# Memory's norm moved behind its transposes, its gain loaded as 8 rows and turned by TensorE, the rotary angles computed on POOL

## The reference

```python
def rms_norm(x, g):
    y = x * lax.rsqrt(jnp.mean(x * x, axis=-1, keepdims=True) + EPS)
    return y * g

def memory_attention(q_flat, mem_n, w_kv):
    kv = (mem_n @ w_kv).reshape(b, n_mem, 2, M_HEADS, M_HEAD_DIM)
    k, v = kv[:, :, 0], kv[:, :, 1]
    ...

mem_n = rms_norm(mem, g_mem)          # once
for l in range(DEPTH):
    h = rms_norm(x, g_mix[l])
    # h @ w_in[l], rotary(q, positions), rotary(k, positions), memory_attention(qm, mem_n, w_mem_kv[l]) ...
```

## Time and profile before

| what | value |
|---|---|
| median of 3 runs | 1711.03 us (1710.94 to 1711.79) |
| the profiled execution's own time | 1710.64 us |
| its span (first to last instruction) | 1708.9 us |
| TensorE busy | 1690.4 us |
| VectorE busy | 1338.8 us |
| ScalarE busy | 1167.7 us |
| POOL busy | 69.8 us |

### The profile page before, as it was taken

How to read it: one execution, slowest core, us unless ns; L and a number is a source line. 1 busy time by engine, 2 the same in 40 slices (tenths; PEclk the granted TensorE clock), 3 DMA queues, 4 the chain that set the end, 5 groups by cost and what they waited for, 6 DMA issues and landing times.

```text
span 1708.9 us, 26645 instructions
## 1 busy us (share of the span) xinstructions
PE 1690.4 (99%) x8790; PEld 1430.2 (84%) x8790; DVE 1338.8 (78%) x1390; ACT 1167.7 (68%) x1362; POOL 69.8 (4%) x91
## 2 busy tenths in 40 slices
PE   9999999999999999999999999999999999999997
PEld 8977889999988877888888888888888888888886
DVE  7675575455457664879998989999899999899998
ACT  6565644444444655578888787787878888887876
POOL 3000000000000000020000000000000000000020
PEclk9999999999999999999999999999999999999999
DMA  9533468666556433699999999999999999999994
GB/s 348 177 112 113 152 228 302 182 193 184 184 160 197 134 113 113 234 360 395 372 376 392 377 376 395 367 385 392 370 385 381 358 403 373 375 396 367 382 354 163
DMA packets 169910, 496.46 MB, mean 291 GB/s; under 512 B 15584, under 2 KB 17680, under 8 KB 169344
## 3 DMA queue, kind: packets, MB, share of 16 engines
q1 hardware_dynamic: 165168, 480.57, 77.6%
q0 software_dynamic: 4688, 15.18, 2.8%
HBM read 482.56 MB, written 13.13 MB: 290 GB/s over the span
## 4 chain that ended last, share of the span: by engine, by line
PE 91%; ACT 3%; DVE 3%; issue 1%; DMA 1%; SPq 0%; DVEq 0%; POOL 0%; ACTq 0%
PE ps L1879 85%; PE ps L2360 1%; ACT probs L1137 1%; PE ps L2161 1%; PE ps L2144 1%; ACT probs L1129 1%; PE ps L2131 1%; DVE wlo L1340 1%; DVE row_max L1555 1%; ACT whi L997 1%; DVE probs L1550 1%; DMA raw<-in_w_mem_kv 1%; PE ps L2133 0%; PE ps L2367 0%; ACT gates L1007 0%
## 5 line engine op out<-in xcount | busy, mean ns | idle before, releaser
L1340 DVE TENSOR_TENSOR wlo<-raw,whi 128x1024 fp32r<-128x1024 f32 (+1 forms) x768 | 910.7, 1218 | 273.0 <-ACT whi L997 252.0
L997 ACT ACTIVATE whi<-raw 128x1024 fp32r<-128x1024 f32 (+1 forms) x768 | 801.1, 1058 | 324.4 <-PE ps L1879 310.0
L1879 PE MATMUL ps<-whi,xg_hi 128*128 128x512 f32 x896 | 351.9, 393 | 0.5 <-DVE xg_lo L1769 0.5
L1879 PE MATMUL ps<-wlo,xg_hi 128*128 128x512 f32 x896 | 348.9, 389 | 0.0
L1879 PE MATMUL ps<-whi,xg_lo 128*128 128x512 f32 x896 | 348.7, 389 | 0.0
L1879 PEld LDWEIGHTS ps<-whi,xg_hi 128*128 128x128 f32 x896 | 168.2, 188 | 36.7 <-DVE wlo L1340 3.0
L1879 PEld LDWEIGHTS ps<-wlo,xg_hi 128*128 128x128 f32 x896 | 168.2, 188 | 35.3
L1879 PEld LDWEIGHTS ps<-whi,xg_lo 128*128 128x128 f32 x896 | 168.3, 188 | 33.9
L1879 PE MATMUL ps<-whi,actm_hi 128*128 128x512 f32 x448 | 175.8, 392 | 0.0
L1879 PE MATMUL ps<-wlo,actm_hi 128*128 128x512 f32 x448 | 174.6, 390 | 0.0
L1879 PE MATMUL ps<-whi,actm_lo 128*128 128x512 f32 x448 | 174.4, 389 | 0.0
(11 more groups left out here) (342 smaller groups left out, 2189.8 us busy)
## 6 DMA issues: line engine op xcount, KB each, us to landing
raw<-in_w_down_exp SPq DMA_DIRECT2D x216, 512.0 KB, 6.3
raw<-in_w_gate_exp SPq DMA_DIRECT2D x210, 512.0 KB, 5.6
raw<-in_w_up_exp SPq DMA_DIRECT2D x120, 512.0 KB, 5.7
raw<-in_w_in SPq DMA_DIRECT2D x72, 512.0 KB, 3.6
vM<-in_w_up_exp SPq DMA_DIRECT2D x56, 512.0 KB, 5.6
kM<-in_w_up_exp SPq DMA_DIRECT2D x48, 512.0 KB, 5.7
raw<-in_w_gate_dense SPq DMA_DIRECT2D x28, 512.0 KB, 3.7
raw<-in_w_up_dense SPq DMA_DIRECT2D x28, 512.0 KB, 3.9
```

What stands on the lines that cost most here:

```text
L997: s.activation(whi[n % SPLIT][:, 0:w], raw[tile(key)][:, 0:w], ACT.Copy).then_inc(chunk_hi, 1)
L1340: v.tensor_tensor(wlo[n % SPLIT][:, 0:w], raw[tile(key)][:, 0:w], whi[n % SPLIT][:, 0:w].bitcast(F32), ALU.subtract).then_inc(chunk_split, 1)
L1879: ins = mm(o, lhsT, rhs, start=start and i == 0, stop=stop and i == 2, skip_group_check=True)
```

## The change

- Memory is transposed as it is loaded, without its norm. The gain is put on as the transposed memory is copied out of PSUM, where a column of `g_mem` is one number per partition. For this `g_mem` is loaded as 8 rows of 128 (4 KB, issued by ACT), transposed by TensorE and copied by DVE to `mem_gain`.
- The rstd of a memory token is put on later: on the values as one number per partition (`values_out`), on the keys as a row `mem_rows`, the same in every partition, which TensorE makes from two diagonal matrices (`mem_diag`, made by DVE from the rstd) and a matrix of ones (`rstd_rows`). `keys_out` moves from ACT to DVE and multiplies by that row. The row is spilled and brought back as the transposed memory is.
- The first chunk's products go in another order: all high x high first, which wait only for the high part, then high x low, then low x high (`first_keys`).
- ACT and DVE take memory's piece ahead of the chunk's high and low part. ACT squares memory's second half and all of `x` after four chunks and ahead of the other four; DVE makes memory's means and the two diagonals after the fourth low part and ahead of the fifth.
- `reduced_angles` moves to POOL, with three of its steps cut in two (19 instructions). POOL's order becomes: identity, positions and frequencies, mask, angles, memory's two powers, x's gain, the small loads, x's powers. x's gain now waits for the two diagonals.
- `idle_products` and the two clearings go; 13 + 7 warming products become 5 + 2 + 2 + 5.

```diff
@@ build_tally
     transposed(("memT",))
+    psum(("mem_rows",), 0)
@@ SP
             for t in range(NT):
                 sp.dma_start(normed[:, t, :], A["mem"][0, P * t:P * (t + 1)]).then_inc(mem_loaded[t], 16)
-            sp.dma_start(gain[:, :], A["g_mem"].partition_broadcast(P)).then_inc(mem_gain_loaded, 16)
...
+                if key == ("qa", 0, 3):
+                    wait_read(sp, ("mem_rows",))
+                    sp.dma_start(rows_spill, mem_rows[:, :]).then_inc(mem_saved, 16)
@@ POOL
-            rstd_of(0)
             (loads of positions and frequencies)
+            (mask: one memset, two affine_selects)
+            reduced_angles()
+            rstd_of(0, mem_rstd)
+            load_gain(1, A["g_mix"][0])
             (small loads, router's weights)
-            (mask: one memset, two affine_selects)
-            load_gain(1, A["g_mix"][0])
@@ POOL, reduced_angles: pool_done adds a wait for the instruction just issued
+                pool_done(nc.gpsimd.tensor_copy(pos_f[:, :], pos_i[:, :]))
+                for t in range(NT):
+                    pool_done(nc.gpsimd.tensor_scalar(ang[:, 2, t, :], freqs[:, :], pos_f[:, t:t + 1], None, ALU.mult))
+                for i, quarter in enumerate((0.0, 0.25)):
+                    pool_done(nc.gpsimd.tensor_scalar(ang[:, 3 + i, :, :], ang[:, 2, :, :], 0.15915494309189535, quarter, ALU.mult, ALU.add))
...
+                pool_done(nc.gpsimd.tensor_scalar(k, k, ROUND, None, ALU.add))
+                pool_done(nc.gpsimd.tensor_scalar(k, k, ROUND, None, ALU.subtract))
+                pool_done(nc.gpsimd.tensor_scalar(ang_part[:, :, :], k, -TWO_PI_HI, None, ALU.mult))
+                pool_done(nc.gpsimd.tensor_tensor(r, ang_part[:, :, :], angle, ALU.add))
...
@@ ACT
+            eng.dma_start(mem_gain_rows[:, :], A["g_mem"].rearrange("(k p) -> k p", p=P)).then_inc(mem_gain_loaded, 16)
+            def mem_hi(i):
+                wait_full(eng, ("memT", i // 2, "area"))
+                for k in range(2 * i, 2 * (i + 1)):
+                    c = TOK * (k % 4)
+                    ins = s.activation(memT_hi[:, k, :], ps[i // 2][:, c:c + TOK], ACT.Copy, scale=mem_gain[:, k:k + 1])
+                ins.then_inc(hi_copied, 1)
...
+            mem_square(0)
+            eng.wait_ge(mem_gain_ready, 1)
+            for i, key in enumerate(opening[0:4]):
+                mem_hi(i)
                 hi_of(key)
+            mem_square(1)
             eng.wait_ge(x_loaded, 16)
+            eng.wait_ge(meansq_ready, NT)
             for t in range(NT):
                 for half in range(2):
                     square(x, half, t)
-            hi_of(opening[6])
-            keys_out(0)
-            hi_of(opening[7])
+            for key in opening[4:]:
+                hi_of(key)
@@ DVE
-            norm(0, normed, normed)
+            v.memset(mem_ones[:, :], 1.0).then_inc(mem_ones_ready, 1)
+            eng.wait_ge(mem_gain_turned, 1)
+            v.tensor_copy(mem_gain[:, :], ps[2][:, 0:KD]).then_inc(mem_gain_ready, 1)
+            eng.wait_ge(mem_gain_ready, 1)
             for i, key in enumerate(opening[0:4]):
+                (two scalar_tensor_tensor: memT_lo = ps * mem_gain - memT_hi)
                 lo_of(key)
-                transposed_piece(("memT",), i, memT_hi, memT_lo)
-            reduced_angles()
+            for t in range(NT):
+                norm_mean(0, t)
+            eng.wait_ge(constants, 3)
+            for t in range(NT):
+                eng.wait_ge(rstd_ready, t + 1)
+                v.tensor_scalar(mem_diag[:, t, :], ident[:, :], mem_rstd[:, t:t + 1], None, ALU.mult).then_inc(norm_done, 1)
             for key in opening[4:6]:
                 lo_of(key)
             wait_full(eng, ("memT", 1, "area"))
             norm(1, x, normed)
+            wait_full(eng, ("mem_rows",))
+            v.tensor_copy(mem_rows[:, :], area(("mem_rows",))[:, 0:TOK]).then_inc(psum_free[0], 1)
+            wait_read(eng, ("mem_rows",))
+            keys_out(0)
             for key in opening[6:] + mixer_chunks(0)[0:2]:
                 lo_of(key)
@@ DVE, layer 0, ahead of the dense block (keys_out(1) was on ACT between two high parts)
+                    lo_of(dense_first[2])
+                    eng.wait_ge(mem_back, 48)
+                    keys_out(1)
+                    lo_of(dense_first[3])
@@ TensorE
             pe.wait_ge(constants, 3)
-            keep_busy(13, ps[3][:, 0:P])
-            pe.wait_ge(tiles_cleared, 2)
-            idle_products()
-            transposes(("memT",), 0)
-            keep_busy(7, ps[3][:, 0:P])
-            for c in range(4):
+            keep_busy(5, ps[3][:, 0:P])
+            pe.wait_ge(mem_gain_loaded, 16)
+            nc.tensor.transpose(ps[2][:, 0:KD], mem_gain_rows[:, :], ident[0:KD, 0:KD]).then_inc(mem_gain_turned, 1)
+            keep_busy(2, ps[3][:, 0:P])
+            transposes(("memT",), 0, [0])
+            keep_busy(2, ps[3][:, 0:P])
+            transposes(("memT",), 0, [1])
+            keep_busy(5, ps[3][:, 0:P])
+            first_keys()
+            for c in range(1, 4):
                 wait_piece(("memT",), c)
                 mem_keys(0, c)
...
                     mem_values(l, c)
+                    if l == 0 and c == 0:
+                        rstd_rows()
```

More of the change, by code:

```diff
@@ new lines, in _ @@
+            reduced_angles()
+            rstd_of(0, mem_rstd)
+            load_gain(1, A["g_mix"][0])
+            for l in range(DEPTH):
+                pool.dma_start(g_lat[:, l, 0:Q_RANK], A["g_q_lat"][l].partition_broadcast(P)).then_inc(small_loaded, 16)
+                pool.dma_start(g_lat[:, l, Q_RANK:], A["g_kv_lat"][l].partition_broadcast(P)).then_inc(small_loaded, 16)
+                pool.dma_start(sink[:, l, :], A["sink"][l].partition_broadcast(P)).then_inc(small_loaded, 16)
+            pool.dma_start(wr[:, :, :], A["w_router"][0].rearrange("(k p) e -> p k e", p=P)).then_inc(router_loaded, 16)
@@ L1024, in transposed, with mem_square @@
                     transposed_part(name, a, dst)
-            for t in range(NT):
+            eng.dma_start(mem_gain_rows[:, :], A["g_mem"].rearrange("(k p) -> k p", p=P)).then_inc(mem_gain_loaded, 16)
[5 more added lines that the diff above has]
+                ins.then_inc(hi_copied, 1)
+            def mem_square(t):
                 eng.wait_ge(mem_loaded[t], 16)
@@ new lines, in _ @@
+            eng.wait_ge(mem_gain_ready, 1)
+            for i, key in enumerate(opening[0:4]):
+                eng.wait_ge(hi_copied, tl.after("hi_copied", ("memT", i)))
+                for k in range(2 * i, 2 * (i + 1)):
+                    c = TOK * (k % 4)
+                    ins = v.scalar_tensor_tensor(memT_lo[:, k, :], ps[i // 2][:, c:c + TOK], mem_gain[:, k:k + 1],
+                                                 memT_hi[:, k, :].bitcast(F32), ALU.mult, ALU.subtract)
+                ins.then_inc(hT_split, 1)
+                lo_of(key)
@@ L1989, in mem_values, with first_keys, rstd_rows @@
                                   banks(("memv", l), 512), 2, 512, c == 0, c == 3))
+            def first_keys():
+                key = ("memk", 0, 0)
+                n = slot(key) % SPLIT
+                o = area(("memk", 0))
+                for i, (w, rows) in enumerate(((whi, memT_hi), (whi, memT_lo), (wlo, memT_hi))):
+                    if i == 0:
+                        pe.wait_ge(chunk_hi, chunk_no(key, 0) + 1)
+                        pe.wait_ge(hi_copied, tl.after("hi_copied", ("memT", 0)))
+                    elif i == 1:
+                        wait_piece(("memT",), 0)
+                    else:
+                        wait_chunk(key)
+                    for kk in range(2):
+                        for j in range(4):
+                            ins = mm(o[:, TOK * j:TOK * (j + 1)], w[n][:, 512 * kk + P * j:512 * kk + P * (j + 1)],
+                                     rows[:, kk, :], start=i == 0 and kk == 0 and j % 2 == 0, stop=False,
+                                     skip_group_check=True)
+                used(ins)
+            def rstd_rows():
+                key = ("mem_rows",)
+                wait_free(pe, key)
+                pe.wait_ge(mem_ones_ready, 1)
+                pe.wait_ge(norm_done, NT)
+                for t in range(NT):
+                    ins = mm(area(key)[:, P * t:P * (t + 1)], mem_ones[:, :], mem_diag[:, t, :], start=True, stop=True)
+                ins.then_inc(psum_full[0], 1)
             def wait_piece(name, i):
```

120 lines of the change are left out of this document (53 added, 67 removed).

## The result

The changed kernel takes 1716.18 us (median of 9 runs, 1715.42 to 1716.91), the kernel before 1711.74 (9 runs, 1710.63 to 1712.12): ratio 1.0028, 95% interval [1.0020, 1.0037], slower by 4.4 us. The profiled execution took 1716.25 us, its span is 1714.5, against 1710.64 and 1708.9. The forecast was 1714.3, with slower a little less likely than no change: the time came out 1.9 above it, inside the range.

The account below looks back on a forecast made before the run. TensorE, busy 99% of the span, was taken as the bound, so c6's start decides: T 23.8 plus 12.2 gives 36.0 against 32.70, 3.3 late. 1710.64 becomes 1713.9, plus 0.39 is 1714.3 us; 8-in-10 range 1708.5 to 1720.

Parts of the forecast that it names:

- first product: TensorE's first real product in the opening, claimed at 8.4 us instead of 13.96, a head start of 5.5 us.
- c4: Fifth of eight memory chunks, c0 to c7; its products claimed at T + 1.2, after TensorE stands idle about 5 us.
- T: End of VectorE's two diagonals, claimed at 23.8 us by the angle chain, against 18 by the sums.
- c6: Seventh memory chunk; its first products claimed at 36.0 us against 32.70, 3.3 late, which shifts the kernel's end.
- interference: VectorE's low parts 0 to 3 stopping POOL's angle chain while they run, claimed at 4.1 us.
- from T to c6: Gain's landing 6.5, x's scaling 2.6, row copy 0.3, keys 1.4, low part 1.2; with two waits 12.2 us.
- chain by itself: POOL's 19 angle instructions, 6.9 us, with 18 waits, 2.7: claimed 9.6 us, bounds 5.8 and 14.4.
- the other path that the prediction named: After T, POOL issues the gain, small loads and the router's, then makes x's powers; the gain can't matter below 6.0 us.
- Slow return of TensorE: Rival: TensorE's clock falls after a standstill; hidden before c4, adding up to 1.4 us before c6, 1715.7; chance 0.07.
- Two standstills: TensorE idle about 5 us before c4 and about 5 before c6 less the transposes, losing the head start.
- Parts at nothing: Angles off VectorE, small loads, row's spill and return, layer 1's keys on VectorE, values as two scalings (0.1): priced near nothing.
- Quick chain: Rival: angle chain ends at 16.8, T at 18.2, c6 at 29.9, 2.8 us early, 1708.2; chance 0.18.

Follow-up runs that it names:

- the doubled chain: Changed kernel with the angle chain on POOL computed twice in the same place: 1728.64 us, ratio 1.0102 to the kernel before.
- the experiment on the start: Changed kernel with its 14 warming products split 11, 0, 0, 7 instead of 5, 2, 2, 5: 1716.64 us, ratio 1.0032 to the kernel before.
- the version without the wait: Changed kernel with angles behind x's powers, x's gain loaded by SP, warming products 11, 0, 0, 7 and VectorE's order packed: 1708.16 us, ratio 0.9981.
- the angles on VectorE: Changed kernel with the angles computed on VectorE again, behind the two diagonals and ahead of the fifth low part: 1712.53 us, ratio 1.0008.
- x's gain freed: Changed kernel with x's gain loaded by SP behind x, x's powers ahead of the small loads, 18 identity products in TensorE's standstill: 1713.49 us, ratio 1.0014.
- The first experiment, angles last: Changed kernel with POOL computing the angles behind x's powers and ScalarE taking their sine later: 1711.64 us, ratio 1.0003 to the kernel before.
- both together: Changed kernel with the angles behind x's powers and x's gain loaded by SP behind x, without the 18 identity products: 1708.55 us, ratio 0.9986.

## Why the prediction was right, and where its sizes were off

The mechanism held point by point: first product early, a standstill of about 5 us before c4 behind a low part that follows a diagonal, POOL's angle rows stretched where low parts run, powers behind the chain, loads behind T, keys on VectorE ahead of c6's low part. The time is as near as it is partly because errors went both ways: a chain 2.4 us too short and a landing 1.1 too early stand against 0.7 too much of interference and 1.2 too much from T to c6. The sizes, in us:

| step | forecast | measured |
|---|---|---|
| first product | 8.4 | 10.63 |
| end of keys 0 | 20.1 | 22.83 |
| chain's start (frequencies landed) | 8.7 | 9.77 |
| chain by itself | 9.6 | 12.0 |
| stopped by VectorE | 4.1 | 3.0 to 3.4 |
| chain's end | 22.4 | 25.14 |
| T | 23.8 | 26.54 |
| from T to c6 | 12.2 | 11.0 |
| c6 | 36.0 | 37.54 |
| span behind c6, more than before | 0 | 0.8 |

- *The mis-sized term is the chain by itself*: 12.0 for 9.6, within its bounds of 5.8 and 14.4. I priced eight one-input rows of 192 columns at 0.36; in the second pass of the doubled chain five take 0.69, two 0.87 and one 0.35, 5.5 us instead of 2.9. I priced a wait at 0.15 and it is 0.08 to 0.09, which gives 1.3 us back. The price was taken near the quick end, by two rows of 0.29 us, a product of two narrow inputs and a select. With the later landing (1.07) and the smaller interference, T comes out 2.7 late.
- *Interference* was sized a little too large, 4.1 for 3.0 to 3.4, by the rows 0.55 and 1.56 of a one-column power. SBUF — State Buffer of the Trainium skill, "Who interferes with whom", has this exclusion as a rule; the doubled chain agrees, 1.55 us beside a low part and 0.69 without. By GPSIMD Engine Reference of the Trainium skill, section 3.1, a two-input addition of 2048 elements takes 1.96 times VectorE's time; measured on 192 columns are 0.59 against 0.36, 1.6 times, and 0.69 against 0.26 for one input, 2.7 times. The estimate from it had given the same 9.6, and was too low where the chain is made of one-input steps.
- *From T to c6*: the gain landed after 4.7 us, not 6.5, so the other path that the prediction named, POOL's issues and x's powers, ended last at T + 6.2. Behind it the two scalings took 2.0 more instead of 2.6, since the first began before the second power was there.
- *The first product* at 10.63 came 2.2 later than forecast. ScalarE waited 2.86 us for memory's first transposes, until 8.79, then took its piece of memory and only then, at 9.52, c0's high part; the prediction had the high part begin when c0 lands, and put the transposes at nothing. Some of it is chance: the same instructions brought the first product at 9.42 to 10.63 in seven kernels. It cost nothing, as the experiment on the start shows. In the version without the wait 0.8 us of start came back as 0.9 of c6.
- *Slow return of TensorE*: the granted clock did fall to 0.50 after the standstill, and c4 took 5.10 us where c5 took 2.74. With it kept at 1.00 the time is the same: the fall lies under VectorE's path, as the prediction had it for c4; before c6 there was no second standstill. As a mechanism this rival is real all the same: it cost 0.8 us with the chain doubled and 1.4 in the profiled executions with the angles on VectorE and with x's gain freed.
- *Two standstills* were forecast, of 5 us and of 5 less the transposes. There was one of 4.9. The second was filled: c4 and c5 came later and slower, and their products lasted until the transposes could begin.
- *Parts at nothing*: with the chain and the gain out of the way no wait in TensorE's list points at the keys, the copied row or the small loads. The high part first is worth 0.45 to 0.9 once nothing stands behind it.
- *Quick chain*: with an early T alone the prediction gave 2.8 us faster. The first experiment has that T and came out even, because under load the gain takes 8.3 us. That rival was priced with x's powers at T + 6.0; by the 7.6 us of the earlier trace rows it would have been 1.6 later, and by the 8.3 of that run c6 comes at 18.8 + 8.3 + 5.7 = 32.8, where 32.89 was measured.

Open remains the 0.8 us behind c6, which grow in small steps (5.2 at 258 us, 5.3 at 740, 5.6 at the end); no wait names them, and in the other kernels they are between 0.2 and 0.9.

## What to carry to other kernels

When an engine off the critical path takes over work, look at what stands behind that work in its list, and put the short steps that others wait for ahead of the long chain. The same chain that cost 4.5 us ahead of two powers left no wait of TensorE's in the opening when it stood behind them. Where two waits lie in series, removing one may only bring the kernel back to even and removing both below it, so ask what is late next before a part of a change is called useless. And ask whether the matrix engine has room behind a standstill: with room its slow return costs nothing, without it it adds to the standstill.

## What the runs showed of the hardware

- POOL against VectorE on 128x192 float32: one input 0.69 against 0.26 us, two inputs 0.59 against 0.36, a comparison with a product 0.87 against 0.26 to 0.39, a minimum with a maximum 0.35 against 0.26 to 0.33. A two-input addition was quicker on POOL than a one-input one.
- The exclusion works both ways: a low part of VectorE that takes 1.22 us by itself took up to 1.61 beside the angles, and 1.22 to 1.23 where POOL was idle (angles last):

```profile
16.59 1.61 DVE L1397 TENSOR_TENSOR wlo<-raw,whi 128x1024 fp32r<-128x1024 f32 x1
```

- The granted clock fell to half after 4.9 us of standstill, also after 2.86 us (the angles on VectorE: products of 0.39 become 0.63 us), and stayed at 1.00 over 1.79 us (angles last). It also fell where 18 identity products and then 1.81 us of standstill lay before c4 (x's gain freed: 0.50 from 30 to 32 us, products of 0.63), and not where the same 18 products and 1.24 us lay before it. So the length of the last standstill alone doesn't tell. Where it fell, c4 took 4.4 to 5.1 us instead of 2.7 to 2.85.
- The first 22 warming products took 4.32 to 5.06 us in different runs of the same instructions, which moves the first real product by as much.
- On POOL's queue a broadcast of 4 KB into 512 KB landed after 4.7 us when the other loads had thinned out and after 8.3 between weights; 24 KB took 5.7 to 7.0 us between weights. On SP's queue, behind x, the same broadcast took 12.4 us (both together).
